# A pooling and neighbourhood-attention encoder layer on eight cores: loads of one buffer issued without order among them, and a rearranged prologue

## The chip, the cores and the metric

The kernel runs on the 8 cores of one Trainium2 chip. Each core computes one batch element, with no exchange between cores. The metric is the device time of the slowest core in microseconds; the time before is the median of 3 runs.

## The reference

One encoder layer over two inputs per core, 8192 and 2048 tokens of 1024 channels. Weights are float32 in DRAM; the kernel multiplies in bf16.

```python
xn = rmsnorm(x, norm_mix); z = xn @ w_in              # 512 p, 512 q, 512 k, 512 v, 2048 gates
g_pool, g_na = split(sigmoid(g + b_gate))
pooled = centred means (windows 2, 4, 8, 16) of p, minus p
pool_out = ((pooled @ w_pool_grp) * pool_scale) @ w_pool_proj
na_out = neighbourhood_attention(q, k, v, rpb) @ w_na_proj   # 8 heads, window 8 rows x 16 columns
x = x + (g_pool * pool_out + g_na * na_out) @ w_out
x = x + square(relu(rmsnorm(x, norm_mlp) @ w_ff1)) @ w_ff2
return rmsnorm(x, norm_final)
```

## The kernel before

**Stages.** A core's 10240 tokens are 20 stages of 512 tokens (stages 0 to 15 the long input, 16 to 19 the short one). A stage is `stage_g` (eight steps m: gate matmuls L801, tanh L806, the two projections L821, the products L825 and L829), `stage_mid` (v_part L557, w_out L874, norms, the next keys L535, p L593, q L704) and `stage_ff` (w_ff1 L937, w_ff2 L964). The attention of the next stage is laid into `stage_ff`: 16 units of head pair and query column group, each a scores matmul (L620), an exponential on ACT (L625), a product with a bias table on DVE (L629) and a values matmul (L643).

**Order of work.** There is no planner. `Prog.op` (L42) appends each instruction to the list of its engine in program order and derives semaphore waits from the keys that it reads and writes. So every engine, and every queue of DMA issues (SP, ACT, POOL), is in order. Two DMAs that write one key get a wait between them: the second is issued when the first has landed. This holds for the two halves of a gate block (`cast_block`, L272), for the two halves of column block 0 in `v_gather` (L571), and for the parts of a bias table in `tab_set` (L378).

**Weights.** All weights pass through a ring of five slots of 1 MB (`wring`), in the order of the list `order`. The first uses of a block are cast from float32 DRAM by POOL (L274); at use number `keep_at` the block is stored to `wbs` by ACT's queue (`keep_block`, L277), and later uses are loaded by SP (L433). BK, BV, BP and BQ are kept at their second use, which falls into stage 0; the blocks of w_ff at the second or third. A slot is filled again when its block has been used and stored. BPP, the pooling projection, is folded with w_pool_grp and pool_scale by `fold` (L1085) into xn2T, and stored.

**Bias tables.** `t_load` brings rpb strips into gsc (two at a time), `t_exp` exponentiates them into xr, `t_masks` makes masks (in xa), and `t_prod` (L346) multiplies: 6 products a kind. `t_kind(2)` is made in `tab[:, 1]`; kinds 0, 3 and 1 are made in `arena`; each is stored to `tabd`. `t_first` makes the half of kind 0 that the first stage needs. `tab_set` loads what the next stage needs.

**Prologue.** It loads six x tiles, norms and transposes them, makes k, v, p and q (`k_back`, `v_part`, `p_back`, `q_proj`), and then runs the first attention alone, with one unit a step, the values two steps behind, and PSUM pairs 0, 4 and 6. `t_kind(0)`, `pooling(0)`, `t_kind(3)` and `fold` are put in at steps 2, 4 to 6, 8 and 10; `t_kind(1)` follows. x tiles 6 and 7 are loaded after it, since the masks lie in xa.

The functions that the diff touches:

## Time and profile before

| | us |
|---|---|
| median of 3 runs | 4442.44 (4439.35 to 4630.74) |
| profiled execution, its own time | 4432.12 |
| its span, first to last instruction, slowest core | 4430.5 |
| spans of the 8 cores | 4394.7 to 4430.5 |
| busy: PE, DVE, ACT, POOL | 4243.8, 2046.5, 1406.4, 481.6 |

Times in rows are microseconds from the start of the span on the slowest core (core 7). PE is the matmul engine, PEld its weight load, DVE the vector engine, ACT the scalar engine, POOL GpSimd; SPq, ACTq are issues of DMAs by those engines. L801 is line 801 of the kernel before. DMA share is the mean busy share of the core's 16 DMA engines. PEclk is the granted clock of PE, 1.00 at the higher of its levels.

### The profile page before, as it was taken

What the parts mean: (1) busy time and instruction counts of PE and PEld (TensorE: products, weight loads), DVE (VectorE), ACT (ScalarE), POOL (GpSimd) and SP (SyncE); (2) the same over time, 40 slices, a digit from 0 to 9 for tenths busy, and PEclk for the clock granted to TensorE, in tenths of its full rate; (3) what the DMA queues carried; (4) which work ended last, traced back from release to release, by engine and by line L of the source; (5) the groups of instructions that cost most, each with busy time, mean ns of one, the idle gap of its engine ahead of it and who ended that gap; (6) DMA issues with size and microseconds to landing.
All of it is one profiled execution on the core that took longest, in us unless ns stands there. A gap on an engine that the chain in (4) does not pass through costs nothing.

```text
span 4430.5 us, 65741 instructions; the slowest of 8 cores (4394.7 to 4430.5 us)
## 1 busy us (share of the span) xinstructions
PE 4243.8 (96%) x23436; PEld 2067.1 (47%) x23436; DVE 2046.5 (46%) x3041; ACT 1406.4 (32%) x2153; POOL 481.6 (11%) x624
## 2 busy tenths in 40 slices
PE   4689899999999999999999999999999999999999
PEld 2334444444444444444444444444444444444544
DVE  3534435344444444444444454544555444444543
ACT  2323323233332333333333332323333232333321
POOL 1021202010101010110101010101010101010100
PEclk8789999999999999999999999999999999999999
DMA  9798887854454544454545454544545454545443
GB/s 177 192 204 179 174 185 203 226 195 172 176 185 156 196 162 174 168 196 164 188 157 194 149 200 159 191 170 176 197 169 179 176 180 177 198 162 180 165 163 123
DMA packets 201832, 790.53 MB, mean 178 GB/s; under 512 B 16360, under 2 KB 99304, under 8 KB 132520
## 3 DMA queue, kind: packets, MB, share of 16 engines
q1 hardware_dynamic: 133352, 695.98, 44.5%
q0 software_dynamic: 64128, 60.99, 10.3%
q10 hardware_dynamic: 4032, 29.36, 1.7%
q8 instruction: 193, 3.16, 0.3%
q14 instruction: 127, 1.04, 0.1%
HBM read 758.47 MB, written 88.78 MB: 191 GB/s over the span
## 4 chain that ended last, share of the span: by engine, by line
PE 89%; DMA 7%; DVE 2%; issue 1%; ACT 1%; SPq 0%; POOL 0%; DVEq 0%; ACTq 0%; POOLq 0%
PE psum L964 24%; PE psum L937 24%; PE psum L801 11%; PE psum L874 6%; PE psum L821 6%; PE psum L620 3%; PE psum L557 3%; PE psum L535 3%; PE psum L704 3%; PE psum L593 3%; PE psum L643 2%; DMA wring<-w_ff 2%; DMA vtok<-vd 1%; PE psum L493 1%; DMA gsc<-rpb 1%
## 5 line engine op out<-in xcount | busy, mean ns | idle before, releaser
L964 PE MATMUL psum<-wring,arena 128*128 128x512 bf16 x5120 | 1160.5, 380 | 12.6 <-DMA wring<-w_ff 12.6
L937 PE MATMUL psum<-xn2T,wring 128*128 128x512 bf16 x5120 | 1163.8, 381 | 4.4 <-DMA wring<-w_ff 3.4
L964 PEld LDWEIGHTS psum<-wring,arena 128*128 128x128 bf16 x5120 | 491.1, 98 | 553.1 <-issue 21.0
L937 PEld LDWEIGHTS psum<-xn2T,wring 128*128 128x128 bf16 x5120 | 492.4, 98 | 547.4 <-issue 16.8
L944 DVE TENSOR_TENSOR arena<-rl 128x512 bf16<-128x512 f32 x640 | 473.2, 741 | 578.0 <-ACT rl L942 577.1
L942 ACT ACTIVATE rl<-psum 128x512 f32<-128x512 f32 x640 | 382.3, 597 | 762.5 <-PE psum L937 603.8
L801 PE MATMUL psum<-xnT,wring 128*128 128x512 bf16 x2560 | 607.8, 380 | 0.0
L625 ACT ACTIVATE pTs<-psum 128x1024 bf16<-128x1024 f32 x320 | 327.4, 1023 | 837.1 <-PE psum L620 810.2
L969 DVE TENSOR_TENSOR xr<-psum,xr 128x512 f32<-128x512 f32 x320 | 221.3, 692 | 621.1 <-PE psum L964 613.2
L472 POOL TENSOR_SCALAR var<-ssq 128x1 f32<-128x1 f32 x240 | 66.8, 278 | 3255.2 <-ACT xs L469 3251.5
L806 ACT ACTIVATE gsc<-psum,hbT 128x512 f32<-128x512 f32 x320 | 218.9, 686 | 541.3 <-PE psum L801 504.2
L801 PEld LDWEIGHTS psum<-xnT,wring 128*128 128x128 bf16 x2560 | 250.3, 98 | 298.9 <-issue 2.8
L629 DVE TENSOR_TENSOR pTs<-pTs,tab 128x1024 bf16<-128x1024 bf16 x320 | 240.9, 753 | 212.4 <-ACT pTs L625 212.4
L825 DVE SCALAR_TENSOR_TENSOR gsc<-gsc,psum 128x512 f32<-128x512 f32 x320 | 216.6, 685 | 235.8 <-PE psum L821 123.4
L874 PE MATMUL psum<-wring,arena 128*128 128x512 bf16 x1280 | 291.7, 387 | 24.3 <-DMA wring<-w_out 11.4
L469 ACT ACTIVATE xs<-xr 128x1024 bf16<-128x1024 f32 x160 | 168.4, 1054 | 226.4 <-DVE xr L969 130.7
L874 PEld LDWEIGHTS psum<-wring,arena 128*128 128x128 bf16 x1280 | 126.0, 99 | 178.4 <-issue 37.0
L620 PE MATMUL psum<-qbd,kT 128*128 128x256 bf16 x1280 | 198.6, 279 | 9.1 <-DVE qbd L466 6.7
L643 PE MATMUL psum<-vtok,pTs 128*128 128x65 bf16 x2560 | 133.5, 196 | 58.8 <-DVE pTs L629 27.3
L475 POOL TENSOR_TENSOR rstd<-var,nhalf 128x1 f32<-128x1 f32 x240 | 183.6, 765 | 37.7 <-POOL var L472 3.4
L643 PEld LDWEIGHTS psum<-vtok,pTs 128*128 128x128 bf16 x2560 | 122.0, 99 | 139.1 <-issue 72.0
L821 PE MATMUL psum<-arena,wring 128*128 128x512 bf16 x640 | 164.2, 379 | 14.9 <-ACT gsc L806 14.9
(88 smaller groups left out, 3036.1 us busy)
## 6 DMA issues: line engine op xcount, KB each, us to landing
wring<-wbs SPq DMA_DIRECT2D x483, 1024.0 KB, 6.0
wring<-w_ff POOLq DMA_DIRECT2D x42, 1024.0 KB, 18.9
xr<-x SPq DMA_DIRECT2D x80, 512.0 KB, 9.0
y<-xr SPq DMA_DIRECT2D x80, 512.0 KB, 3.7
xa<-x SPq DMA_DIRECT2D x76, 512.0 KB, 6.8
wbs<-wring ACTq DMA_DIRECT2D x27, 1024.0 KB, 11.3
xn2T<-wbs SPq DMA_DIRECT2D x19, 1024.0 KB, 7.4
vd<-vst SPq DMA_DIRECT2D x19, 520.0 KB, 8.4
```

Of the source, the lines that this page charges most:

```text
L620: ins = e.matmul(out=pb(pair + rb, lr * 256, lr * 256 + 256), lhsT=kT[:, m, ks, cb, :], rhs=qbd[:, m, g, :, :], start=True, stop=True)
L625: P.op("act", lambda e: e.activation(out=pTs[:, pslot, :], in_=psum[:, pair * 512:pair * 512 + 1024], func=AF.Exp, scale=0.125), reads=["p ...
L629: P.op("dve", lambda e: e.tensor_tensor(out=pv_, in0=pv_, in1=tab[:, :, v0:v0 + 2, 2 * m:2 * m + 2, :].rearrange("p r v h q -> p r v (h q) ...
L643: ins = e.matmul(out=pb(bo, ocol, ocol + 65), lhsT=pTs[:, pslot, base:base + 128], rhs=vtok[:, ks, cb, h, :], start=(i == 0), stop=(i == 3))
L801: ins = e.matmul(out=pb2(b), lhsT=WG[:, k, col0:col0 + 128], rhs=xn(u0, k), start=(k == 0), stop=(k == 7))
L821: ins = e.matmul(out=pb(b2), lhsT=Wp[:, k, m * 128:(m + 1) * 128], rhs=src[:, k, :], start=(k == 0), stop=(k == 3))
L874: ins = e.matmul(out=pb(b), lhsT=mT[:, k, tl * 128:(tl + 1) * 128], rhs=W[:, k, :], start=(k == 0), stop=(k == 7))
L937: ins = e.matmul(out=pb(b), lhsT=W[:, k, c4 * 128:(c4 + 1) * 128], rhs=xn2T[:, k, :], start=(k == 0), stop=(k == 7))
L942: P.op("act", lambda e, b=b, rs_=rs_: e.activation(out=rl[:, rs_, :], in_=pb(b), func=AF.Relu), reads=["ps%d" % b], writes=["rl%d" % rs_])
L944: P.op("dve", lambda e, rs_=rs_, hc=hc: e.tensor_tensor(out=hidT[:, hc, :], in0=rl[:, rs_, :], in1=rl[:, rs_, :], op=ALU.mult), reads=["rl ...
L964: ins = e.matmul(out=pb(b), lhsT=hidT[:, kg * 8 + k, tl * 128:(tl + 1) * 128], rhs=W[:, k, :], start=(kg == 0 and k == 0), stop=(kg == 1 a ...
L969: P.op("dve", lambda e, b=b, xv=xv: e.tensor_tensor(out=xv, in0=pb(b), in1=xv, op=ALU.add), reads=["ps%d" % b, "xr%d" % tl], writes=["xr%d ...
```

## The change

Four things are changed. (1) `op` takes `joined`: such a DMA does not wait for others on its own semaphore. It is used for the later parts in `cast_block`, `v_gather` and `tab_set`. (2) BK, BV, BP and BQ are kept at their first use, in the prologue. (3) The masks move out of xa into xr and arena, kinds are all made in `tab`, kinds 1, 3 and 0 in the first `stage_g` after steps m = 0, 1 and 3, each stored by `t_keep`; since kinds 0 and 1 are then in place, stage 0 reloads no table. (4) Loads and prologue are reordered: six x tiles first, strips and small constants behind; wgn, BQ, BPP, and x tiles 6 and 7 before `k_back`; `t_exp(0)` and `(1)` after it, `t_exp(2)` and `(3)` after v; `q_proj` ahead of `t_kind(2)`; `fold` ahead of the first attention, in which only the pooling is left, one operation list entry per step from step 3.

```diff
-    def op(self, eng, fn, reads=(), writes=(), dsem=None):
+    def op(self, eng, fn, reads=(), writes=(), dsem=None, joined=False):
...
+        own = self.dsems[dsem][0] if joined else None
...
             s, v, clk = tok
+            if s is own:
+                return
...
-        for (vf, src) in block_srcs(b):
+        for i, (vf, src) in enumerate(block_srcs(b)):
             P.op("pool", lambda e, vf=vf, src=src: e.dma_start(out=vf(dst), in_=src, max_dma_last_dim=8192),
-                 writes=[wkey], dsem=wkey)
+                 writes=[wkey], dsem=wkey, joined=i > 0)
...
-    masks = xaf[:, 0:1536].bitcast(BF16).rearrange("p (k v q) -> p k v q", k=4, v=6)
+    masks = [(xr[:, 3, 384 * k:384 * k + 384].bitcast(BF16) if k < 2 else arena[:, 4608 + 768 * k:5376 + 768 * k])
+             .rearrange("p (v q) -> p v q", v=6) for k in range(4)]
+    MSK = ["mk%d" % k for k in range(4)]
...
     def t_kind(k):
+        rb = (0, 1, 1, 0)[k]
         for v in range(6):
-            t_prod(k, dst, keys, 0, 128, v)
+            t_prod(k, tab[:, rb], ["tab%d" % rb], 0, 128, v)
+
+    def t_keep(k):
+        rb = (0, 1, 1, 0)[k]
+        P.op("sp", lambda e: e.dma_start(out=tabd[k], in_=tab[:, rb].rearrange("p v h q -> p (v h q)")),
+             reads=["tab%d" % rb], writes=["tabd%d" % k], dsem="tabd%d" % k)
...
-                        reads=["tabd%d" % k], writes=[key], dsem=key)
+                        reads=["tabd%d" % k], writes=[key], dsem=key, joined=key in begun)
+                    begun.add(key)
...
-    keep_at.update({b: 1 for b in (BK, BV, BP, BQ)})
...
-                    reads=["vd%d" % blk] + (["vd0"] if blk == 0 else []), writes=["vtok%d_%d" % (ks, cb)], dsem="vt%d_%d" % (ks, cb))
+                    reads=["vd%d" % blk] + (["vd0"] if blk == 0 else []), writes=["vtok%d_%d" % (ks, cb)], dsem="vt%d_%d" % (ks, cb),
+                    joined=lo > 0)
...
-    x_load(0)
-    load(g1b[:], norm_mix.partition_broadcast(128), "g1b")
-    x_load(1)
-    x_load(2)
-    x_load(3)
+    for j in range(6):
+        x_load(j)
+        if j == 0:
+            load(g1b[:], norm_mix.partition_broadcast(128), "g1b")
+    t_load(0)
+    t_load(1)
+    load(psT[:], pool_scale, "psT")
     load(mrow[:], c_mrow, "mrow")
     load(mcol[:], c_mcol, "mcol")
-    t_load(0)
-    t_load(1)
-    x_load(4)
-    x_load(5)
+    load(bgT[:], b_gate, "bgT")
+    load(pfac[:], c_fac, "pfac")
...
     p_norm(1)
-    ws_fill(1)
     a_tr(0)
     p_norm(2)
     a_tr(1)
     p_norm(3)
-    t_first_zero()
     ws_fill(1)
-    t_exp(0)
-    t_exp(1)
-    t_load(2)
-    t_load(3)
+    P.op("pool", lambda e: e.dma_start(out=wgn, in_=w_grp.rearrange("g c d -> c g d"), max_dma_last_dim=8192), writes=WGN, dsem="wgn")
+    ws_fill(2)
+    for j in (6, 7):
+        a_load(j)
...
         p_norm(5)
-        t_exp(2)
-        t_exp(3)
         a_tr(4)
         a_tr(5)
+        t_first_zero()
         t_masks()
     k_back([0, 1], rest)
-    P.op("pool", lambda e: e.dma_start(out=wgn, in_=w_grp.rearrange("g c d -> c g d"), max_dma_last_dim=8192), writes=WGN, dsem="wgn")
+    t_exp(0)
+    t_exp(1)
+    t_load(2)
+    t_load(3)
...
-    load(psT[:], pool_scale, "psT")
-    load(bgT[:], b_gate, "bgT")
-    load(pfac[:], c_fac, "pfac")
+    t_exp(2)
+    t_exp(3)
...
     t_first()
+    q_proj(0)
     t_kind(2)
-    q_proj(0)
+    t_keep(2)
...
+    fold()
     reserved.update((2, 3))
     P.fence("act", ["xp4", "xp5"])
     plan = att_plan(0, 1, 2, [0, 4, 6])
-    plan[2].append(lambda: t_kind(0))
-    plan[4].append(lambda: pool_fin.extend(pooling(0)))
-    plan[6].append(lambda: [f_() for f_ in pool_fin])
-    plan[8].append(lambda: t_kind(3))
-    plan[10].append(fold)
+    for i, f_ in enumerate(sum(pooling(0), [])):
+        plan[i + 3].append(f_)
...
-    t_kind(1)
+    tab_now.update({(0, 0): 0, (0, 1): 0, (1, 0): 1, (1, 1): 1})
+    g_hooks[0] = [lambda: t_kind(1), lambda: t_keep(1)]
+    g_hooks[1] = [lambda: t_kind(3), lambda: t_keep(3)]
     g_hooks[2] = [lambda: keep_block(xn2f, BPP, "xn2T")]
+    g_hooks[3] = [lambda: t_kind(0), lambda: t_keep(0)]
     load(g2b[:], norm_mlp.partition_broadcast(128), "g2b")
     load(nfb[:], norm_final.partition_broadcast(128), "nfb")
-    for j in (6, 7):
-        a_load(j)
```

## Rows read from the trace of the kernel before

**Rows 1.** The page, busy tenths in 40 slices of the span (DMA: mean share)

```profile
PE   4689899999999999999999999999999999999999
...
DMA  9798887854454544454545454544545454545443
```

**Rows 2.** Timeline of PE, first gate matmuls of stages; start us, us, form

```profile
164.77 3.62 PE L801 MATMUL psum<-xnT,wring 128*128 128x512 bf16 x8
...
415.34 1.89 PE L801 MATMUL psum<-xnT,wring 128*128 128x512 bf16 x8
...
649.85 1.89 PE L801 MATMUL psum<-xnT,wring 128*128 128x512 bf16 x8
...
1080.46 1.89 PE L801 MATMUL psum<-xnT,wring 128*128 128x512 bf16 x8
...
1290.11 1.89 PE L801 MATMUL psum<-xnT,wring 128*128 128x512 bf16 x8
...
3388.90 1.89 PE L801 MATMUL psum<-xnT,wring 128*128 128x512 bf16 x8
...
3608.77 1.89 PE L801 MATMUL psum<-xnT,wring 128*128 128x512 bf16 x8
```

**Rows 3.** Stretches: length, busy PE PEld DVE ACT POOL, PEclk, DMA share, GB/s

```profile
120.00:150.00 30.00, 11.91 (x88) 7.14 (x88) 20.51 (x39) 8.24 (x10) 0.86 (x1) 0.53 0.33 115
300.00:390.00 90.00, 88.69 (x526) 44.09 (x524) 43.23 (x68) 29.50 (x43) 13.47 (x14) 1.00 1.08 156
480.00:640.00 160.00, 140.62 (x793) 68.89 (x792) 63.47 (x92) 44.98 (x67) 25.54 (x24) 0.93 1.00 186
```

**Rows 4.** Timeline of PE, its waits; in brackets idle before and its releaser

```profile
109.59 0.60 PE L643 MATMUL psum<-vtok,pTs 128*128 128x65 bf16 x8 [14.03 <-DVE pTs L629]
...
236.51 3.57 PE L874 MATMUL psum<-wring,arena 128*128 128x512 bf16 x8 [5.06 <-DMA wring<-w_out]
...
293.03 0.60 PE L643 MATMUL psum<-vtok,pTs 128*128 128x65 bf16 x8 [3.94 <-DMA vtok<-vd]
...
519.23 0.60 PE L643 MATMUL psum<-vtok,pTs 128*128 128x65 bf16 x8 [12.22 <-DMA vtok<-vd]
...
633.93 3.57 PE L964 MATMUL psum<-wring,arena 128*128 128x512 bf16 x8 [7.17 <-DMA wring<-w_ff]
...
3443.27 3.57 PE L874 MATMUL psum<-wring,arena 128*128 128x512 bf16 x8 [5.53 <-DMA wring<-wbs]
```

**Rows 5.** Timeline of DVE in the first attention, same columns

```profile
81.90 10.92 DVE L348 TENSOR_TENSOR tab<-xr,xa 64x1024 bf16<-64x1024 bf16 x14
...
108.15 0.17 DVE L1083 TENSOR_SCALAR hbT<-bgT 128x16 f32<-128x16 f32 x1 [12.78 <-DMA bgT<-b_gate]
...
112.87 4.67 DVE L348 TENSOR_TENSOR arena<-xr,xa 128x1024 bf16<-128x1024 bf16 x6
...
143.28 1.45 DVE L1095 TENSOR_SCALAR rl<-psum,psT 128x128 bf16<-128x128 bf16 x4
...
150.18 0.69 DVE L466 CAST xn2T<-psum 128x512 bf16<-128x512 f32 x1 [0.78 <-ACT xn2T L464]
```

**Rows 6.** Timelines of POOL and of ACT, same columns

```profile
29.97 0.96 POOL L274 DMA_DIRECT2D wring<-w_in  x1 [10.95 <-issue]
...
200.82 1.06 ACT L469 ACTIVATE xs<-xa 128x1024 bf16<-128x1024 f32 x1 [9.06 <-DMA xa<-x]
```

**Rows 7.** DMA queues from 165 to 620: packets, MB, share of 16 engines

```profile
q0 software_dynamic: 39013, 39.35, 63.7%
q1 hardware_dynamic: 8013, 32.23, 22.5%
```

**Rows 8.** Chain that ended last, in order of time: start us, us, what

```profile
282.21 10.68 DMA vtok<-vd
...
504.05 14.94 DMA vtok<-vd
```

**Rows 9.** Timeline of SP's queue: start us, us from first issue to last

```profile
3417.50 15.38 SPq L401 DMA_DIRECT2D tab<-tabd  x5
```

More of the change, by code:

```diff
@@ L312, in build_nc @@
     VST = ["vst%d" % c for c in range(6)]
-    xaf = xa[:].rearrange("p a b -> p (a b)")
-    masks = xaf[:, 0:1536].bitcast(BF16).rearrange("p (k v q) -> p k v q", k=4, v=6)
-    XA = ["xa0", "xa1"]
+    masks = [(xr[:, 3, 384 * k:384 * k + 384].bitcast(BF16) if k < 2 else arena[:, 4608 + 768 * k:5376 + 768 * k])
+             .rearrange("p (v q) -> p v q", v=6) for k in range(4)]
+    MSK = ["mk%d" % k for k in range(4)]
     expb = xr[:].rearrange("p a b -> p (a b)")[:, 0:3072].bitcast(BF16).rearrange("p (h q) -> p h q", h=24)
@@ L334, in t_masks @@
                 P.op("dve", lambda e, k=k, v0=v0, v1=v1, ty=ty: e.tensor_tensor(
-                    out=masks[:, k, v0:v1, :].rearrange("p v (r q) -> p v r q", q=16),
+                    out=masks[k][:, v0:v1, :].rearrange("p v (r q) -> p v r q", q=16),
                     in0=mrow[:, k, ty, :].unsqueeze(1).unsqueeze(3).broadcast_to([128, v1 - v0, 8, 16]),
                     in1=mcol[:, v0:v1, :].unsqueeze(2).broadcast_to([128, v1 - v0, 8, 16]), op=ALU.mult),
-                    reads=["mrow", "mcol"], writes=XA)
+                    reads=["mrow", "mcol"], writes=[MSK[k]])
     def ex_view(o, rb):
@@ L349, in t_prod @@
             out=dst[lo:lo + n, v], in0=ex_view(VAR_OFF[v], rb)[lo:lo + n],
-            in1=masks[lo:lo + n, k, v, :].unsqueeze(1).broadcast_to([n, 8, 128]), op=ALU.mult),
-            reads=EXPB + XR4 + XA, writes=keys)
+            in1=masks[k][lo:lo + n, v, :].unsqueeze(1).broadcast_to([n, 8, 128]), op=ALU.mult),
+            reads=EXPB + XR4 + [MSK[k], "hid12", "hid13", "hid14"], writes=keys)
     def t_kind(k):
-        if k == 2:
-            dst, keys = tab[:, 1], ["tab1"]
-        else:
-            dst = arena[:, 0:6144].rearrange("p (v h q) -> p v h q", v=6, h=8)
-            keys = HID
-        for v in range(6):
-            t_prod(k, dst, keys, 0, 128, v)
-        P.op("sp", lambda e: e.dma_start(out=tabd[k], in_=dst.rearrange("p v h q -> p (v h q)")),
-             reads=keys, writes=["tabd%d" % k], dsem="tabd%d" % k)
+        rb = (0, 1, 1, 0)[k]
+        for v in range(6):
+            t_prod(k, tab[:, rb], ["tab%d" % rb], 0, 128, v)
[3 more added lines that the diff above has]
+             reads=["tab%d" % rb], writes=["tabd%d" % k], dsem="tabd%d" % k)
     def t_first_zero():
@@ L374, in t_first @@
             t_prod(0, tab[:, 0], ["tab0"], 96, 32, v)
-    tab_now = {(0, 0): None, (0, 1): 0, (1, 0): 2, (1, 1): 2}
+    tab_now = {}
     def tab_set(first, last):
@@ L391, in tab_set @@
             todo += [(rb,) + p_ for p_ in parts]
+        begun = set()
         for zero in (True, False):
@@ L739, in pooling, with sum2, double @@
         eng = "dve" if s == 0 else "pool"
-        P.op(eng, lambda e: e.tensor_tensor(out=sm, in0=p(1, 4, -8, 526), in1=p(1, 4, -7, 526), op=ALU.add),
-             reads=win, writes=GSC)
-        for i, d in enumerate((2, 4, 8)):
-            n = (524, 520, 512)[i]
-            P.op(eng, lambda e, i=i, d=d, n=n: e.tensor_tensor(out=sm[:, i:3, 0:n], in0=sm[:, i:3, 0:n],
-                                                                in1=sm[:, i:3, d:d + n], op=ALU.add),
+        def sum2():
+            P.op(eng, lambda e: e.tensor_tensor(out=sm, in0=p(1, 4, -8, 526), in1=p(1, 4, -7, 526), op=ALU.add),
+                 reads=win, writes=GSC)
+        def double(i):
+            d, n = (2, 4, 8)[i], (524, 520, 512)[i]
+            P.op(eng, lambda e: e.tensor_tensor(out=sm[:, i:3, 0:n], in0=sm[:, i:3, 0:n],
+                                                in1=sm[:, i:3, d:d + n], op=ALU.add),
                  reads=GSC, writes=GSC)
+        sums = [sum2] + [lambda i=i: double(i) for i in range(3)]
         def fin0():
@@ L763, in fin @@
                 op0=ALU.mult, op1=ALU.add), reads=win + GSC, writes=["pooledT"])
-        return [fin0] + [lambda g=g: fin(g) for g in range(1, 4)]
+        return sums, [fin0] + [lambda g=g: fin(g) for g in range(1, 4)]
     def x_res(s):
@@ L909, in stage_mid @@
             q_proj(s + 1)
-            pool_fin[:] = pooling(s + 1)
+            sums, pool_fin[:] = pooling(s + 1)
+            for f_ in sums:
+                f_()
     def stage_ff(s):
@@ L1010, in build_nc @@
     ws_fill(2)
-    P.op("dve", lambda e: e.memset(nhalf[:], -0.5), writes=["nhalf"])
-    x_load(0)
-    load(g1b[:], norm_mix.partition_broadcast(128), "g1b")
-    x_load(1)
-    x_load(2)
-    x_load(3)
+    for j in range(6):
[5 more added lines that the diff above has]
+    load(psT[:], pool_scale, "psT")
     load(mrow[:], c_mrow, "mrow")
     load(mcol[:], c_mcol, "mcol")
-    t_load(0)
-    t_load(1)
-    x_load(4)
-    x_load(5)
+    load(bgT[:], b_gate, "bgT")
+    load(pfac[:], c_fac, "pfac")
     P.op("dve", lambda e: e.memset(xnT[:, :, 0:256], 0.0), writes=["xnT0"])
```

## The prediction

> **What bounds the kernel now.** I read the 40 slices first [rows 1]. PE is at 9 tenths from the sixth slice on; the first five (some 550 us) hold 4, 6, 8, 9, 8. The DMA line stands at 7 to 9 through the first eight and then falls to 4 and 5. So two regimes: a start in which the DMA engines are full, and a steady part bound by PE. Next the first gate matmul of each stage, from the timeline of PE [rows 2]. Between 1080.46 and 1290.11 a stage takes 209.7 us; that is PE's own length, and what a stage takes beyond it is what could be gained. The prologue ends at 164.8. Stage 0 takes 415.3 - 164.8 = 250.5 (40.8 beyond), stage 1 649.8 - 415.3 = 234.5 (24.8 beyond), stage 15 219.9 (10.2); the next is of the same pattern (8.0). These two are the ones that reload bias tables in parts. Third, the stretches [rows 3]: at 120 to 150 PE is busy 11.9 of 30 us at half clock (0.53) while DMA is at 0.33, DVE is busiest (20.5); at 300 to 390 and 480 to 640 DMA is at 1.08 and 1.00, no room. Last the waits of PE in the timeline [rows 4] and DVE's own line through the first attention [rows 5].
>
> **Prologue and first attention.** Before, the first values matmul waits 14.03 us for DVE and starts at 109.59 [rows 4], because DVE sat 12.78 us on b_gate, whose load was queued behind the gathers, until 108.15 [rows 5]. After, b_gate is loaded at the head, so that wait is gone, but other things stand there. In DVE's new order are: the eight products of t_first and six of t_kind(2) (10.92 us for the 14, [rows 5]), with q's four copies (2.5 us) between; fold's four scalings (1.45) and its eight copies of xn2T, a chain that alternates ACT and DVE and takes 0.73 us a link and 5.9 in all, the last at 150.18; then scores, exp and product, some 3 us. Sum 23.8 us, with hbT 24. It starts when p's copies are done, 81.9 before. That now waits for t_exp(2) and t_exp(3), which stand ahead of them on ACT and whose bias strips can only be loaded once t_exp(0) and (1) have freed gsc, after k_back; DVE then also has t_first_zero (4.6) and t_masks (6.2) between the two K blocks, so k's last copy goes from 61 to about 64, t_exp(0) ends at 65.5, two loads of 0.75 MB take 10 to 14 us there, and p's copies end at 87. 87 + 24 = 111 for the first values matmul, 1.5 us later than before. So the b_gate wait is not gained; it is refilled.
>
> The gain is in the attention. It took 164.8 - 109.6 = 55.2 us. Two t_kinds of 4.67 us and fold (143.28 to 150.87 with PE's part and the stall behind it, 10 us) stood in DVE's line [rows 5]; with lag 2 and three PSUM pairs little of that is hidden. 55.2 - 9.3 - 10 = 36. The pooling, spread over eight units where it came in two lumps, hides some 3 us more: 33. Prologue end 111 + 33 = 144, **-21 us**. Bounds: if the strips land early and DVE's other work hides, 133 (-32); if they land as t_load did in a full queue, and POOL holds the norms of tiles 4 and 5 behind BPP, 158 (-7). That POOL can be held is in the row at 29.97: the fourth cast of a block waited 10.95 us with nothing before it but queue space [rows 6]; now wgn, BQ and BPP all stand before those two norms. I take 2 us for it, within the 87.
> K, V, P, Q are stored to wbs already here: four stores of 1 MB, 3.3 us of all DMA engines each (below). They delay slots 0 to 3, but the casts of BG0 to BG2 are due only at 144, and DMA was idle for two thirds of 120 to 150 [rows 3]; hidden by that.
>
> **Stage 0.** Price of DMA work from 165 to 620 [rows 7]: the software queue (casts) 39.35 MB in 63.7% of 455 us, 7.4 us per MB, 7.7 per block of 1.05 MB; the hardware queue 32.23 MB in 22.5%, 3.2 per MB, 3.3 per block. BV, BK, BP, BQ become plain loads: 4 x 4.4 = 18 us less, their stores are past: 13 less; no table reload (2.36 MB): 7.5 less; tiles 6 and 7 loaded in the prologue: 3 less; tables 1, 3 and 0 are written here, where only 1 was: 2 x 1.57 MB, 10 more. Net 31 us of DMA work less, in a stage where the share was full to 390. Now place by place, against 40.8 us excess. (a) Gates: 214.7 - 164.8 = 49.9 for 41.4 of work; 6 us were the waits for tiles 6 and 7, the table product and slow clock. After, three t_kinds of 4.67 us stand in DVE's line after m = 0, 1 and 3, and the third writes the buffer that t_keep(3) is still reading (7 to 13 us for 1.5 MB), so DVE waits some 4 us, with the products of m = 4 and the evacuations behind it. PE runs two m ahead through 8 banks; I leave 5 us of stall, gain 1 to 2. (b) v_part and w_out: PE waited 2.4 us, then 5.06 at 236.51 and 6.36 at the one like it before, and ran eight matmuls twice in 3.57 us where 1.73 is full speed, 17.5 in all [rows 4]. BWO0 was late because its slot waited for the store of BG1, whose issue sat on ACT behind the norm of a late tile; that one goes. BWO1 stays: ACT still waits for tile 8 (9.06 us before [rows 6], loaded behind t_keep(3) on SP now), so the store of BG2 lands at +42 and the cast 16 to 20 us later, against a need at +50. I leave 10 us, gain 7.5. (c) The gather: PE waited 3.4 + 3.9 us around 280 to 293 for the second half of a pair that was issued when the first had landed (10.7 us later [rows 8]); joined, both land together. With the clock (6.35 and 6.15 us for 16 matmuls, 3.45 at speed) 13 us, of which 12 go. **-21 us** (a + b + c, 20.5 to 21.5). Is DMA ready? Before, BWO's release at 250 to the last ff cast at 392 was 142 us, with 11 us to spare at the end; PE now needs 13 less, DMA has 5 to 6 less there. It just fits, and from here the bound is close. Bounds -8 to -34.
>
> **Stage 1.** The same gather costs 12.22 us at 519.23, the longest wait [rows 4], the second half landing 14.94 us after the first [rows 8]. But 480 to 640 is full of DMA: 16 casts x 7.7 = 123, six stores and some loads of 3.3, together about 155 of 160 us, and PE waits again at 633.93, 7.17 us, for the last ff blocks. Taking 12 us out moves that wait up, it does not remove it: what is gained is the DMA idle time that PE's stall made (520 to 530), **-4 us**, bounds 0 and -16.
>
> Here the Trainium skill speaks otherwise. The last rows have a gather half of 65 KB landing 10.7 us after issue in a full queue [rows 8]. "DMA: Bandwidth & Descriptors" (Anatomy of one DMA) fits a DMA with 2.0 us plus bytes over 436 GB/s. An estimate by that page is 2.2 us for the half, so joining would give 2 us a stage, and a block of 1 MB would take 4.4, so that 16 would fit well under PE. By it stage 0's gather would give 2 us instead of 12, and the sum be 10 less there and up to 8 more in stage 1. The rows decide; the rest stands on them.
>
> **Stages 15 and 16, and all others.** At 3417.5 SP needs 15.38 us to issue five table loads [rows 9], each waiting for the one before; the wring load behind them makes PE wait 5.53 us at 3443.27 with 3.57 for eight matmuls [rows 4] (the same at 3663). Joined, five issues take 3 us, so the load goes 12 us earlier: 7.5 each, **-15 us** (bounds -10, -17). In the other stages SP is freed for 4.5 us each, and nothing waits there: 0.
> Sum -21 -21 -4 -15 = -61: 4432.1 - 61 = 4371 of this execution, whose span is 4430.5. The median of the runs shown is 10.3 us higher; the prediction is for that: 4442.4 - 61, 4381.
>
> **Rivals.** (1) DMA takes it back. Work moved forward meets casts that can't come sooner: stage 0's last blocks are late by what the front gained. For it: DMA 1.08 to 390 [rows 3]. Against: 31 us less work, and idle time at 120 to 150 that can be used. The prologue's 21 stays half, stage 0 gives 5: -10 -5 -0 -15 = -30, 4412. (2) All of it comes through: prologue -32, stage 0 -34, stage 1 -14 (casts not the bound), tables -17: -97, 4345. The fit of the Trainium skill above would have it so for the casts. For it: the waits that go are there in full, 14.03, 3.94 and 12.22 us [rows 4]. Against: the wait for w_ff at 633.93. (3) The joined loads do not help, since the second half lands when it did anyhow, in a queue that is served in turn: -61 + 12 + 4 + 5 = -40, 4402. (4) Slower. One mechanism: a slot can be refilled only after its block was stored, the stores are issued by ACT, and ACT sits on strips loaded late; then BG1 to BG3 are late in the gates, and every later block in a ring without slack. A hold of ACT for one late tile was 9.06 us [rows 6]; nine such landing on PE (four slots in the gates, five while the ring catches up in stages 0 and 1) are 81.5. It decides from the seventh on, 61 us: -61 + 81 = +20, 4462. DMA's idle 120 to 150 speaks against it.
>
> **Chances.** Forecast 0.60, (1) 0.16, (2) 0.14, (3) 0.07, (4) 0.03. The range is 4345 to 4422: it takes in (1), (2) and (3). A measurement here tells 2% (89 us) from no change: faster by that is under 4353.6, most of (2) and a little of the forecast, 0.13; slower 0.02; within 0.85.
>
> **What would show it.** First values matmul at 111 with no 12.78 us wait for b_gate; gates from 144; attention 33 us; b_gate, fold and two t_kinds outside it. PE's wait for w_out once, near 10 us. In stage 0 no wait for vtok over 3 us; in stage 1 vtok gone and the w_ff wait near 634 grown to 15 or more after the shift. SP's five table loads in 3 us and no wait at stages 15 and 16. It is wrong if gates start after 155, if stage 1 takes under 222 us (then casts did not bind), or if stage 0 stays over 240.

## The result, and the profile after

The changed kernel takes 0.989 of the time before (95% interval 0.986 to 0.993): 48 us less of 4442, between 33 and 63. The prediction was 61 us less. The medians of all runs are 4396.34 and 4536.59 us; executions in which the cores of a die ran at a lower clock pull the second one up, and the ratio leaves them out. The profiled execution took 4394.56 us (before 4432.12), its span is 4392.7 us, on core 1.

The page after, the same lines as [rows 1]:

```profile
PE   5689989899999999999999999999999999999999
...
DMA  9898988845454545454545454545455554545443
```

The first slices are fuller (5, 6, 8, 9, 9 against 4, 6, 8, 9, 8), and the DMA line of the first eight is as full as it was. The steady part is the same. The first gate matmuls of the stages, as in [rows 2] (L808 is L801 before):

```profile
149.88 3.62 PE L808 MATMUL psum<-xnT,wring 128*128 128x512 bf16 x8
...
395.07 1.89 PE L808 MATMUL psum<-xnT,wring 128*128 128x512 bf16 x8
...
626.79 1.89 PE L808 MATMUL psum<-xnT,wring 128*128 128x512 bf16 x8
...
851.15 1.89 PE L808 MATMUL psum<-xnT,wring 128*128 128x512 bf16 x8
...
1060.94 1.89 PE L808 MATMUL psum<-xnT,wring 128*128 128x512 bf16 x8
...
3369.09 1.89 PE L808 MATMUL psum<-xnT,wring 128*128 128x512 bf16 x8
...
3580.46 1.89 PE L808 MATMUL psum<-xnT,wring 128*128 128x512 bf16 x8
```

Prologue 149.9 (164.8 before), stage 0 245.2 (250.5), stage 1 231.7 (234.5), stage 2 224.4 (220.9), a steady stage 209.8 still, stage 15 211.4 (219.9).

The slowest core is not the same one in every trace, and stages 0 to 2 differ from core to core by up to 20 us (stage 1 before: 214.7 to 234.5), so the experiments are read by the median over the eight cores, taken from the same first gate matmuls in each core's trace:

| medians over 8 cores, us | prologue | stage 0 | 1 | 2 | 15 | 16 | slowest span |
|---|---|---|---|---|---|---|---|
| before | 161.9 | 253.7 | 221.7 | 220.8 | 218.2 | 217.7 | 4430.5 |
| changed | 149.9 | 243.2 | 227.0 | 221.4 | 211.4 | 210.0 | 4392.7 |
| e1_before_joined | 159.0 | 256.3 | 223.8 | 221.6 | 211.4 | 209.9 | 4415.2 |
| e2_after_unjoined | 149.1 | 248.3 | 226.6 | 221.9 | 216.4 | 217.4 | 4423.0 |
| e3_early_stores | 149.8 | 239.2 | 229.9 | 218.8 | 211.4 | 209.9 | 4387.9 |
| e4_no_table_stores | 151.0 | 231.4 | 229.5 | 222.3 | 211.4 | 209.9 | 4384.8 |
| e6_late_keep | 148.5 | 259.3 | 223.4 | 221.3 | 211.4 | 210.0 | 4401.2 |
| e7a_after_ff_plain | 148.4 | 244.1 | 209.7 | 209.7 | 211.4 | 209.9 | 4358.5 |
| e7b_before_ff_plain | 163.2 | 255.5 | 209.7 | 209.7 | 217.8 | 217.4 | 4405.5 |
| e8_early_strips | 143.6 | 245.7 | 229.9 | 219.7 | 211.4 | 210.0 | 4386.9 |
| e9_keep_split | 149.5 | 255.1 | 214.9 | 211.9 | 211.4 | 209.9 | 4381.3 |
| e10_three | 144.5 | 247.5 | 211.8 | 211.8 | 211.4 | 209.9 | 4369.9 |
| e11_three_half | 145.6 | 262.0 | 209.7 | 209.7 | 211.4 | 209.9 | 4376.0 |
| e12_four | 145.3 | 232.4 | 214.4 | 211.8 | 211.4 | 209.9 | 4368.0 |

By it the change gave 12 us in the prologue and 10.5 in stage 0, lost 5.3 in stage 1 and 0.6 in stage 2, and gave 14.5 in stages 15 and 16. The rest is mostly the slowest core: before, the latest of the eight was 11.6 us behind the median core (4430.5 against 4418.9), after, 6.7. A median hides where the cores fall into two groups; where they do (e9, e10, e12), the text says so.

**The prologue.** Timeline of DVE after, where [rows 5] was:

```profile
86.63 0.42 DVE L469 CAST pTb<-psum 128x256 bf16<-128x256 f32 x1 [13.82 <-ACT pTb L467]
...
90.29 6.22 DVE L351 TENSOR_TENSOR tab<-xr 64x1024 bf16<-64x1024 bf16 x8
...
99.09 4.67 DVE L351 TENSOR_TENSOR tab<-xr,arena 128x1024 bf16<-128x1024 bf16 x6
...
103.88 1.46 DVE L1104 TENSOR_SCALAR rl<-psum,psT 128x128 bf16<-128x128 bf16 x4
...
111.35 0.69 DVE L469 CAST xn2T<-psum 128x512 bf16<-128x512 f32 x1 [0.78 <-ACT xn2T L467]
```

The 12.78 us wait for b_gate is gone, and what has taken its place is the 13.82 us wait for p's copies on ACT. Then follow t_first (6.22), q's copies, t_kind(2) (4.67), fold's scalings, and the copies of xn2T, the last at 111.35. ACT waited itself, for the strips (timeline of ACT):

```profile
80.07 1.49 ACT L330 ACTIVATE xr<-gsc 128x1536 bf16<-128x1536 f32 x1 [9.11 <-DMA gsc<-rpb]
84.78 1.48 ACT L330 ACTIVATE xr<-gsc 128x1536 bf16<-128x1536 f32 x1 [3.23 <-DMA gsc<-rpb]
```

and POOL was held at the issue of a cast, as in the row at 29.97 of [rows 6], here twice: 10.25 us before 30.48, and then (timeline of POOL):

```profile
45.80 0.75 POOL L277 DMA_DIRECT2D wring<-w_pool_proj  x1 [14.43 <-issue]
```

The cast of BPP waited 14.43 us with two norms behind it. The profile names no releaser, but by the trace's landings both casts went out 0.3 us after an earlier one had landed (30.14 and 45.49), which is what a wait for queue space looks like. The first of the two norms reached DVE at 47.73, where tile 4's stood at 43.70 before.

**PE's waits** after, for [rows 4] (timeline of PE, in brackets the idle time before and its releaser):

```profile
115.79 0.60 PE L647 MATMUL psum<-vtok,pTs 128*128 128x65 bf16 x8 [1.63 <-DVE pTs L633]
...
209.17 3.03 PE L560 MATMUL psum<-wring,xnT 128*128 128x512 bf16 x8 [3.68 <-DVE gsc L832]
...
230.22 3.57 PE L881 MATMUL psum<-wring,arena 128*128 128x512 bf16 x8 [15.34 <-DMA wring<-w_out]
...
276.31 0.40 PE L647 MATMUL psum<-vtok,pTs 128*128 128x65 bf16 x8 [1.42 <-DMA vtok<-vd]
...
523.06 3.57 PE L973 MATMUL psum<-wring,arena 128*128 128x512 bf16 x8 [5.29 <-DMA wring<-w_ff]
...
611.75 3.57 PE L973 MATMUL psum<-wring,arena 128*128 128x512 bf16 x8 [10.22 <-DMA wring<-w_ff]
```

The first values matmul is at 115.79, 6.2 us later than before. The second w_out block makes PE wait 15.34 us. The gathers cost 1.42 us in stage 0 and nothing in stage 1, where the w_ff blocks cost 5.29 and 10.22. That is not the slowest core alone: in stage 1 before, all eight cores waited for vtok, 3.2 to 12.2 us, and three of them for w_ff (7.2, 7.1 and 0.8 us); after, one waits for vtok (1.6 us at most), and all of them for w_ff, 8.1 to 10.9 us at the last blocks. In stage 0 the waits for w_out come to as much as before: 15.5 us before in the median over the cores, in two waits, and 15.3 after, on most cores in one. The slowest core of the kernel before had the smallest sum of the eight, 11.4 us. Where the 15.34 us come from, in the chain that ended last:

```profile
171.91 16.33 DMA xa<-x
...
188.71 15.53 DMA wbs<-wring
...
204.98 25.10 DMA wring<-w_out
```

Tile 8 loads for 16.3 us, the store of BG2 that ACT issues after it takes 15.5, the cast into the slot 25.1. ACT's wait for the tile (timeline of ACT):

```profile
188.61 1.06 ACT L472 ACTIVATE xs<-xa 128x1024 bf16<-128x1024 f32 x1 [13.69 <-DMA xa<-x]
```

And the stretches (columns as in [rows 3]):

```profile
150.00:165.00 15.00, 15.00 (x59) 6.27 (x58) 7.48 (x12) 4.82 (x9) 0.72 (x2) 0.83 0.25 99
165.00:180.00 15.00, 15.00 (x82) 7.26 (x81) 11.27 (x16) 3.71 (x6) 2.19 (x4) 1.00 1.02 299
180.00:195.00 15.00, 9.42 (x33) 3.52 (x32) 8.49 (x12) 5.18 (x9) 0.79 (x2) 0.81 1.04 279
195.00:210.00 15.00, 11.32 (x50) 4.91 (x49) 4.16 (x7) 2.65 (x4) 1.75 (x3) 0.96 1.02 266
210.00:225.00 15.00, 4.22 (x14) 1.19 (x12) 3.69 (x6) 0.00 (x0) 0.00 (x0) 0.73 1.02 290
```

DMA stands at 0.25 in the first 15 us of the gates and then at 1.02 to 1.04 for 60 us. SP's queue at stage 15, for [rows 9]:

```profile
3397.68 3.09 SPq L404 DMA_DIRECT2D tab<-tabd  x5
3401.60 11.55 SPq L436 DMA_DIRECT2D wring<-wbs  x3
```

Five table loads in 3.09 us instead of 15.38, and no wait of PE behind them.

### The profile page after: what moved, and what is told of

The parts are those of the page before. It is cut to its first block, busy times and chain, and to the rows that moved or that the text cites. A ratio compares the mean times of both kernels' runs of the same rounds, so it can differ in the third digit from the quotient of the medians.

```text
span 4392.7 us, 65696 instructions; the slowest of 8 cores (4370.4 to 4392.7 us)
## 1 busy us (share of the span) xinstructions
PE 4227.1 (96%) x23436; PEld 2061.6 (47%) x23436; DVE 2048.1 (47%) x3040; ACT 1406.2 (32%) x2153; POOL 479.4 (11%) x620
## 3 DMA queue, kind: packets, MB, share of 16 engines
q14 instruction: 127, 1.04, 0.1%
## 4 chain that ended last, share of the span: by engine, by line
PE 91%; DMA 5%; issue 2%; DVE 2%; ACT 1%; POOL 0%; ACTq 0%; SPq 0%; DVEq 0%; POOLq 0%
PE psum L973 25%; PE psum L946 23%; PE psum L808 12%; PE psum L881 6%; PE psum L828 6%; PE psum L538 3%; PE psum L624 3%; PE psum L708 3%; PE psum L560 3%; PE psum L597 3%; DMA wring<-w_ff 2%; PE psum L647 2%; PE psum L496 2%; DMA wbs<-wring 1%; DMA wring<-w_out 1%
## 5 line engine op out<-in xcount | busy, mean ns | idle before, releaser
L808 PE MATMUL psum<-xnT,wring 128*128 128x512 bf16 x2560 | 608.5, 381 | 2.3 <-ACT gsc L813 2.3
L808 PEld LDWEIGHTS psum<-xnT,wring 128*128 128x128 bf16 x2560 | 250.5, 98 | 302.6 <-issue 7.4
L881 PE MATMUL psum<-wring,arena 128*128 128x512 bf16 x1280 | 284.4, 381 | 17.9 <-DMA wring<-w_out 15.3
L828 PE MATMUL psum<-arena,wring 128*128 128x512 bf16 x640 | 164.2, 379 | 18.2 <-ACT gsc L813 14.9
L485 DVE SCALAR_TENSOR_TENSOR xs<-xr,rstd,g2b 128x1024 bf16<-128x1024 f32 x80 | 102.7, 1284 | 143.6 <-POOL rstd L478 140.1
## 6 DMA issues: line engine op xcount, KB each, us to landing
wbs<-wring ACTq DMA_DIRECT2D x27, 1024.0 KB, 11.6
```

The lines of the kernel that those rows point to most:

```text
L808: ins = e.matmul(out=pb2(b), lhsT=WG[:, k, col0:col0 + 128], rhs=xn(u0, k), start=(k == 0), stop=(k == 7))
L828: ins = e.matmul(out=pb(b2), lhsT=Wp[:, k, m * 128:(m + 1) * 128], rhs=src[:, k, :], start=(k == 0), stop=(k == 3))
L881: ins = e.matmul(out=pb(b), lhsT=mT[:, k, tl * 128:(tl + 1) * 128], rhs=W[:, k, :], start=(k == 0), stop=(k == 7))
```

## The experiments

The question after the trace: stage 0 gave 5 to 10 us where 21 were forecast, and stage 1 got longer in the median. Is the second w_out block late because its slot is held (theory D, the way the prediction had worked it out), or because the queues are full (E)? And do the casts of w_ff take back what comes before them (A)?

**e1_before_joined, e2_after_unjoined: the joined loads alone, and all the rest alone.** The edit of e1 is the hunks of the change that have `joined` in them. e2:

```diff
-            if s is own:
-                return
```

> The kernel before with the joined loads alone (gate block halves, gathers, table parts), nothing moved. Theory A (my forecast's steps): the gather wait of stage 0 goes, stage 0 is 10 to 13 us shorter; stage 1 only 0 to 5 shorter, its 12 us wait for vtok comes back as waits for w_ff; stages 15 and 16 are 8 us shorter each; in all -26 to -34 us. Rival B (casts don't bind in the ff phase): stage 1 is 12 to 15 us shorter as well, in all -40 or more. Rival C (joining gives nothing, the second half lands when it did): stages 0, 15 and 16 as before, in all 0 to -5.

> The changed kernel with every joined load waiting for the one before again. Theory A: the prologue is hardly later (first gate matmul within 4 us of 149.9), stage 0 is 8 to 12 us longer, stage 1 within 4 us, stages 15 and 16 8 us longer each, in all +22 to +32 us against the changed kernel, which leaves it 10 to 20 us faster than before. Rival C: within 5 us of the changed kernel.

e1 takes 0.994 of the time before (0.992 to 0.996), 27 us less; e2 0.996 (0.994 to 0.998), 18 us less. Together 45 of the 48: within the intervals the two halves add up. Stages 15 and 16 are as expected, 14.6 us in the medians, and in e2 both rows are back (SP's queue, then PE, at stage 15):

```profile
3410.82 17.03 SPq L402 DMA_DIRECT2D tab<-tabd  x5
```

```profile
3437.76 3.57 PE L879 MATMUL psum<-wring,arena 128*128 128x512 bf16 x8 [6.70 <-DMA wring<-wbs]
```

But stage 0 of e1 missed: 256.3, no shorter than before. Its gather wait is gone, and another has grown (timeline of PE in stage 0 of e1):

```profile
229.87 3.57 PE L880 MATMUL psum<-wring,arena 128*128 128x512 bf16 x8 [17.33 <-DMA wring<-w_out]
...
293.94 0.40 PE L649 MATMUL psum<-vtok,pTs 128*128 128x65 bf16 x8 [0.57 <-DMA vtok<-vd]
```

PE waits 17.33 us for the first w_out block. Over the eight cores this wait is 12.5 to 17.3 us, where it was 6.4 to 9.7 before. In e1's trace SP issues its five table loads at 189.73 within 3.88 us, and the cast of that block goes out behind them at 194.31. That the loads then stand in the queues ahead of it, and that the two edits are better together because the changed kernel has no such loads in stage 0, is argued from these two times and from the medians over the cores (the cast goes out 34.3 us after the start of the gates, 33.7 before, and lands at 68.2, where it was 62.3); it was not tried alone. e2's stage 0 is 5.1 us longer than the changed kernel's, not 8 to 12.

**e3_early_stores, e4_no_table_stores: slot held, or queues full.** The edit of e3:

```diff
+    def keep_ahead(b):
+        kept.add(b)
+        slot = ws["slot_of"][order.index(b)]
+        keep_block(wring[:, slot, :], b, "wr%d" % slot)
...
-        if b != BPP and uses[b] - 1 == keep_at[b]:
+        if b != BPP and uses[b] - 1 == keep_at[b] and b not in kept:
...
+        if s == 0:
+            keep_ahead(BG[1])
+            keep_ahead(BG[2])
```

e4 drops the three `t_keep` calls from the hooks and puts them into stage 6; what is stored for kind 3 is then kind 0, so the tables of the last stages of each input are wrong.

> The changed kernel with the stores of gate blocks BG1 and BG2 issued by ACT at the start of the first gates instead of when each block is taken up. Theory D (w_out is late because its slot waits for a store that ACT issues only after it has sat on the late tile 8): the cast of the second w_out block is issued about 183 to 186 instead of 205, PE's 15.3 us wait for it falls to 0 to 3, stage 0 is 12 to 16 us shorter unless the casts of w_ff then bind; total -8 to -16. Rival E (DMA throughput: table stores and tiles fill the queues): the cast is issued earlier but lands late, the wait falls by less than 6 us, total 0 to -5.

> The changed kernel with the three table stores taken out of the first gates and put into stage 6, where the buffers hold other kinds: what is stored there is wrong, and the tables of the last stages with it. All products stay. Theory D: tile 8 is loaded as early as the gathers of DVE let it, ACT's 13.7 us on it falls to about 9, DVE's 4.5 us wait for the store of kind 3 goes, PE's wait for w_out falls by some 5 us, stage 0 is 6 to 10 us shorter. Rival E: 13.5 us of DMA work less ahead of the w_out casts takes the whole 15 us wait and more away, stage 0 is 14 us shorter or more.

e3 takes 0.989 of the time before (0.987 to 0.991), the same as the changed kernel; e4 0.988 (0.985 to 0.991), which can't be told from it. In e3 the cast was issued 15.7 us earlier (POOL), 3 to 6 us later than D had it, since the norm of tile 8 stands ahead of it on POOL. But PE waits as long (PE):

```profile
189.32 0.96 POOL L277 DMA_DIRECT2D wring<-w_out  x1
```

```profile
206.71 1.89 PE L893 MATMUL psum<-wring,arena 128*128 128x512 bf16 x8 [2.68 <-DMA wring<-w_out]
224.62 3.57 PE L893 MATMUL psum<-wring,arena 128*128 128x512 bf16 x8 [16.02 <-DMA wring<-w_out]
```

189.32 to 224.62 is 35 us in the queue, where it was 25.1. The cast was issued 15.7 us earlier and the block landed 5.6 us earlier; stage 0 is 4.0 us shorter in the median, stage 1 2.9 longer and stage 2 2.6 shorter. D, as it was worked out (wait near zero), falls. In e4 the cast was issued earlier too, 13.1 us (191.87), and here the block landed 13.7 us earlier, 216.47 for 230.22:

```profile
216.47 3.20 PE L881 MATMUL psum<-wring,arena 128*128 128x512 bf16 x8 [14.84 <-DMA wring<-w_out]
```

```profile
210.00:225.00 15.00, 8.53 (x46) 4.13 (x47) 2.77 (x4) 2.06 (x3) 0.79 (x2) 0.69 0.45 118
```

At 210 to 225 the share is down to 0.45. The slowest core is another one in each run, so here are the same two times as medians over the eight cores, with two later runs:

| second w_out block of stage 0, us after the first gate matmul | cast issued | landed |
|---|---|---|
| before | 46.9 | 72.0 |
| changed | 52.3 | 77.6 |
| e3_early_stores | 39.6 | 73.7 |
| e4_no_table_stores | 39.7 | 66.0 |
| e10_three | 46.7 | 70.7 |
| e12_four | 36.4 | 66.9 |

So the same advance of the cast, 12.7 and 12.6 us, passes by a third where the other DMA work stays (e3, 3.9 us), and nearly in full where three table stores are gone (e4, 11.6 us). Three stores of 1.57 MB are some 15 us of DMA work by [rows 7]; the expectation had 13.5. e4 alone would not tell the theories apart, since its cast was early as well; the pair does. E expected e4's wait to go, and it did not: 14.84 us. PE had got there some 13 us earlier itself (201.6 for 214.9), since ACT's wait for tile 8 and DVE's for the store were shorter too. Stage 0 is 11.8 us shorter, somewhat less than the work, and stages 1 and 2 were 3.4 us longer together, so of 12 us 8 were left.

**e7a_after_ff_plain, e7b_before_ff_plain: do the casts bind stages 1 and 2.** The edit, in both kernels:

```diff
-            if order[:i].count(b) <= keep_at[b] and b != BPP or b == BPP:
+            if b >= 12 and order[:i].count(b):
+                P.op("sp", lambda e, slot=slot: e.dma_start(out=wring[:, slot, :], in_=wbs[BG[0]]),
+                     reads=["wbs%d" % BG[0]], writes=["wr%d" % slot], dsem="wl%d" % slot)
+            elif order[:i].count(b) <= keep_at[b] and b != BPP or b == BPP:
...
-        if b != BPP and uses[b] - 1 == keep_at[b]:
+        if b < 12 and b != BPP and uses[b] - 1 == keep_at[b]:
```

> The changed kernel in which every use of a w_ff block after the first is a plain load of another block already stored, and no w_ff block is stored: what the MLP of stages 1 to 19 computes is wrong, the amount of bf16 loaded is that of the steady stages. Theory A (the casts of w_ff bind stages 1 and 2, and take there what the front gained): stages 1 and 2 fall from 227 and 221 us (medians over the cores) to 210 to 213. Stage 0 keeps its 16 casts and stays at 240 to 245. Rival F (stage 1 and 2 are long for another reason, the norms, the attention or the clock): they stay over 218.

> The kernel before with the same w_ff loads (same part wrong). Theory A: stage 1 holds its gather wait here (nothing gives it back), so it stays 6 to 15 us over 209.7; stage 2 falls to 210 to 213; against the changed kernel with the same loads the difference is larger than the 48 us of the two kernels as they are: -50 to -60 us. Rival F: the same 40 to 50 us.

First gate matmuls of stages 1, 2 and 3 in e7a, then of 1 and 2 in e7b (timelines of PE):

```profile
396.08 1.89 PE L811 MATMUL psum<-xnT,wring 128*128 128x512 bf16 x8
...
605.83 1.89 PE L811 MATMUL psum<-xnT,wring 128*128 128x512 bf16 x8
...
815.48 1.89 PE L811 MATMUL psum<-xnT,wring 128*128 128x512 bf16 x8
```

```profile
429.68 1.89 PE L804 MATMUL psum<-xnT,wring 128*128 128x512 bf16 x8
...
639.39 1.89 PE L804 MATMUL psum<-xnT,wring 128*128 128x512 bf16 x8
```

Both stages take 209.7 us in the median over the cores, in both kernels. So all of the 17 and 12 us that they are over the steady length in the changed kernel is the casts and stores of w_ff. The edit takes away their DMA work and POOL's issuing of them at once, so that it is the work, and not the way of issue, is argued: from the DMA share of 1.00 with the casts [rows 3] and from e9 below. The expectation for e7b missed in one thing, and it is the most telling: its gathers still wait for each other, and yet stage 1 has no gather wait.

```profile
480.00:640.00 160.00, 160.00 (x929) 79.50 (x927) 70.12 (x111) 51.93 (x78) 15.19 (x18) 1.00 0.43 155
```

PE is busy 160.00 of 160 us, with DMA at 0.43. The 12.22 us of [rows 4] were a small load behind casts, not the price of a load that waits for another. Changed against before with these loads: 0.983 and 0.994, 10 thousandths or 46 us, no more than between the two kernels as they are; 50 to 60 was expected. The expectations for the stages of e7a held (stage 0 is 244.1).

**e8_early_strips: does a shorter prologue come through.**

```diff
     p_norm(3)
+    t_exp(0)
+    t_exp(1)
+    t_load(2)
+    t_load(3)
     ws_fill(1)
...
     k_back([0, 1], rest)
-    t_exp(0)
-    t_exp(1)
-    t_load(2)
-    t_load(3)
+    t_exp(2)
+    t_exp(3)
...
-    t_exp(2)
-    t_exp(3)
     slot, wkey = ws_acquire(BP)
```

> The changed kernel with t_exp(0), t_exp(1), t_load(2), t_load(3) ahead of the K blocks, and t_exp(2), t_exp(3) right behind them. If the strips' late loads cost the prologue what the profile shows (ACT 9.1 + 3.2 us for rpb, PE 4.3 us for p's copies), the first gate matmul comes 5 to 9 us earlier, 141 to 145 in the median; the total falls by less than that, 0 to 5, if the casts of stages 0 to 2 bind, and by all of it if they don't.

ACT exponentiates the strips at 24 to 30, while it has nothing else, and after the K blocks without a wait (ACT); the gates begin earlier (PE):

```profile
24.35 1.48 ACT L330 ACTIVATE xr<-gsc 128x1536 bf16<-128x1536 f32 x1 [6.42 <-DMA gsc<-rpb]
...
66.10 2.86 ACT L330 ACTIVATE xr<-gsc 128x1536 bf16<-128x1536 f32 x2
```

```profile
144.91 3.62 PE L808 MATMUL psum<-xnT,wring 128*128 128x512 bf16 x8
```

The prologue is 6.3 us shorter in the median. Stages 0 to 2 together are 3.7 us longer, so by the sum of the medians 2.6 came through by the start of stage 3, as A has it (3.8 by the median of the eight start times themselves). There is no ratio for this run, and a gain of that size would not show in one.

**e6_late_keep: the four stores in the prologue.** The edit puts `keep_at.update({b: 1 for b in (BK, BV, BP, BQ)})` back.

> The changed kernel with BK, BV, BP and BQ stored at their second use again (as before the change). Theory A: the prologue is 0 to 3 us shorter (no stores in a full queue, no slot waits for them), and stage 0 6 to 12 us longer, since four casts and four stores return to it: total +3 to +9. Rival: early keeping is worth nothing or costs, total 0 to -5.

0.992 (0.989 to 0.995), some 12 us slower than the changed kernel by the ratios, though their intervals overlap; the median core is 8.5 us later (4394.5 against 4386.0). The prologue is 1.4 us shorter and stage 0 16.1 longer, more than the 6 to 12 expected: four casts for four loads and four stores, some 30 us of work put where no room is. Of all parts undone this one costs stage 0 most: without it the stage would be longer than before the change (259.3 for 253.7).

**e9_keep_split, e10_three, e11_three_half: less DMA work.** If the start of stage 3 is set by DMA work, the way to gain is to take work away. A block of w_ff stored at its first use costs one store in stage 0 and saves one or two casts after it. e9:

```diff
-        keep_at[12 + n_] = 1 if n_ % 3 == 0 else 2
+        keep_at[12 + n_] = (0, 1, 2, 1, 2, 1, 2, 0)[n_ % 8]
```

e10 is that with the edit of e8 and with `t_keep(1)` and `t_keep(0)` moved from stage 0's hooks to stage 6, where their buffers still hold these kinds. e11 is e10 with `n_ % 2`.

> The changed kernel with the stores of the 16 w_ff blocks split over three stages: 4 at the first use, 6 at the second, 6 at the third (before: 6 at the second, 10 at the third). Theory A (total DMA work up to the start of stage 3 sets when stage 3 starts): 4 more stores in stage 0 (4 x 2.7 us), in stage 1 four casts with or without store and in stage 2 eight casts less. Stage 1 falls from 227 to 211 to 217 us, stage 2 from 221 to 210 to 214, stage 0 rises by 3 to 11; total -10 to -20 against the changed kernel. Rival (only the burst in each ff phase counts, stores in stage 0 cost more than they return): total -5 to +5.

> The same split, with the strips loaded and exponentiated early, and with the stores of bias table kinds 1 and 0 put off to stage 6 (their buffers hold them until stage 14, so nothing is left out). Theory A: prologue 143 to 145 us, two table stores of three out of stage 0 (8 of the 12 us that taking out three gave), stages 1 and 2 as in the split alone: total -22 to -32 against the changed kernel, near 4365. Rival: as the split alone, -10 to -20, since the front's gains are taken back again.

> As the last, but 8 blocks stored at the first use and 8 at the second. Theory A: stage 2 is 209.7 us, stage 1 210 to 212, stage 0 6 to 11 us longer than with four stores: total within 6 us of the last, to either side.

e9: 0.986 (0.983 to 0.988), 16 us less than the changed kernel by the ratios, whose intervals overlap; the times themselves, taken on two chips, do not (4373.21 to 4383.53 against 4386.15 to 4398.11). Stage 1 is 214.9, stage 2 211.9, as expected, and stage 0 is 11.9 us longer in the median, a little over the 3 to 11 expected. But the median stands for no core: on two of the eight stage 0 is 241.8 and 242.5, no longer than in the changed kernel, and on six it is 253.1 to 258.5. The six wait 6 to 9 us for one of the last w_ff blocks of the stage, the two don't. e10: 0.984 (0.981 to 0.986), 25 us less than the changed kernel, in the range expected, and again 0.984 (e10b_three, the same kernel). There too stage 0 has two short cores (234.7 and 237.1) and six long ones (242.9 to 251.6). e11: 0.985 (0.983 to 0.987): stages 1 and 2 are at 209.7, and stage 0 is 14.5 us longer than e10's, where 6 to 11 were expected; all eight cores are long (260.0 to 265.9) and wait 20 to 22 us for w_ff blocks. In e10 PE waits in stage 0 for w_out and at the end of w_ff:

```profile
216.21 3.57 PE L881 MATMUL psum<-wring,arena 128*128 128x512 bf16 x8 [13.84 <-DMA wring<-w_out]
...
380.88 3.57 PE L973 MATMUL psum<-wring,arena 128*128 128x512 bf16 x8 [7.71 <-DMA wring<-w_ff]
```

**e12_four, e10b_three: the question of e3 again, with room in the queues.** e10 and the edit of e3.

> The run with three changes (e10) and the early stores of BG1 and BG2 (e3) on top. Theory E (DMA work ahead of the second w_out block sets when it lands; early stores only use the idle DMA of the first gates, 0.34 share at 150 to 165): PE's wait for w_out stays 9 to 15 us, the landing comes 3 to 7 us earlier, stage 0 is 3 to 6 us shorter of which the ff casts take back some; total -2 to -5 against e10. Theory D (the held-up store): with two table stores gone the queues have room at 210 to 225 (0.45), so the wait falls by 8 us or more, total -8.

> The same kernel as e10, for a comparison on the same chip as e12: 0.98 to 0.986 of the kernel before.

```profile
180.91 0.96 POOL L277 DMA_DIRECT2D wring<-w_out  x1
```

```profile
212.44 3.57 PE L893 MATMUL psum<-wring,arena 128*128 128x512 bf16 x8 [14.55 <-DMA wring<-w_out]
```

The cast was issued 10.5 us earlier than in e10, the block landed 3.8 us earlier, and PE's wait is 14.55 us. E again: a third of the advance passed. Stage 0 is 15 us shorter in the median over the cores (232.4), which neither theory expected. It is the two groups again: five cores are short now (230.3 to 233.0, no wait for a w_ff block), where e10 had two, and three are long (245.2 to 248.1, with 8.0 to 8.3 us of such a wait near the end of the stage). So the earlier block may have taken three more cores past that wait, with which a core's stage is some 14 us longer in all; whether it is the cause is open, since one profiled execution can't show that it would be so again. The slowest span, 4368.0, is a long core's and 1.9 us from e10's. e12 takes 0.982 (0.978 to 0.986), e10b on the same chip 0.984 (0.981 to 0.986): they can't be told apart. Both beat the kernel before; their intervals end where the changed kernel's begins, at 0.986.

## Why the prediction was right or wrong

The sum was -61 and -48 was measured. The mechanisms of the prologue and of the table loads were right; one step of stage 0 was not.

**Prologue, -21 forecast, -14.9 on the slowest core (-12.0 in the median).** The mechanism was right and the attention itself too: 149.9 - 115.8 = 34.1 us for a forecast of 33, with two t_kinds and fold taken out of it. The first values matmul was due at 111 and came at 115.8. Two terms were too small: p's copies were done at 90.3, not 87, since the strips were waited for until 84.78 and POOL held the norms 4 us instead of 2; and the chain behind them took 25.5 us, not 24. That b_gate's wait would be refilled rather than gained was right.

**Stage 0, -21 forecast, -5.3 on the slowest core (-10.5 in the median).** By a sign that the prediction named itself (wrong if stage 0 stays over 240) it was wrong here: 245.2. The step that failed is (b), v_part and w_out, a gain of 7.5 us. I had read the lateness of the second w_out block as a chain of issue times (late tile, store, cast) and left 10 us of 17.5. In that chain the store of BG2 was to land 42 us after the start of the gates, the cast 16 to 20 us behind it, and PE to be there at 50. Measured, the store landed at 54.4 (issued at 38.8, in the queue for 15.5), the cast was 25.1 us in the queue and landed at 80.2, and PE was there at 65.0. From the first v_part matmul to the end of that block's first eight matmuls it is 30.2 us, where it was 25.4 (medians over the cores 28.5 and 26.9). So 2 to 5 us were lost where 7.5 were to be gained.

What the chain had too short is the time that a transfer stays in full queues. The issue time counts, but only by a third (e3, e12: medians of 12.7 and 10.3 us of advance gave 3.9 and 3.8); with the table stores gone nearly the whole advance came through (e4). So the landing is set mostly by the other DMA work then in the queues, and there the change puts two more table stores. The 31 us of DMA work that I had counted as gone did go, and the count was right: the share over stage 0 is 1.00 of 250.6 us before and 0.89 of 245.2 us after, 32 us less. But much of it went at times when DMA was then idle (0.25 at 150 to 165) because the five slots were full (POOL's next cast, at 173.06, waited for PE's gates to free one), and up to the start of stage 3 nothing went: 0.88 of 870.7 us before, 0.90 of 851.1 us after, some 766 us of work each time. The change moved DMA work ahead; e9 takes some away (0.86 of 839.1 us, some 720).

(a) failed too, 53.7 us for the gates instead of 48 to 49: DVE waited 4.54 us for the store of kind 3 as forecast, but ACT 13.69 us for tile 8. (c) has the right size, 1.42 us of wait are left, but one of its rows was misread: of the 3.4 + 3.9 us put down to the gather, the first is a wait for a w_ff block.

```profile
282.74 6.35 PE L937 MATMUL psum<-xn2T,wring 128*128 128x512 bf16 x16 [3.43 <-DMA wring<-w_ff]
```

It went too, and joining the gather in the kernel before (e1) did not shorten the stage; so the 14 us by which the stage is shorter from the w_out block on (161.3 for 175.2) are not the gather's alone. A store was priced by the wrong queue, too: ACT's stores are a hardware queue of their own, 16.43 MB in 9.5% of the 455 us of [rows 7], 2.8 us for a block and not 3.3.

**Stage 1, -4 forecast.** On the slowest cores it is -2.8; in the median over the cores +5.3. The reason given held: the wait for vtok went from 12.22 us to none, and the waits for w_ff grew from 7.17 to 15.5 ("15 or more"). e7a shows that the casts and stores of w_ff are all of it. But the prediction let stage 0 pass its gain on. Rival (1), that DMA takes back what the front gains, is in part what happened: 12 + 10.5 us gained ahead of stage 1, 5.9 taken back in stages 1 and 2, and of e8's 6.3 us 2.6 came through. The weight of 0.60 against 0.16 was too one-sided; the measured -48 lies between the -61 of the one and the -30 of the other.

**The weighing of the Trainium skill.** By an estimate from the fit in "DMA: Bandwidth & Descriptors" (Anatomy of one DMA) of the Trainium skill, 16 casts fit well under PE. No run agrees: with casts stages 1 and 2 are 12 to 17 us over, without them 209.7. The Trainium skill gives that fit for DMAs issued by GpSimd; the gather is issued by SP, so the fit was not made for it, and the 2.2 us estimated for a half were 10.68 and 14.94 us in the full queues [rows 8]. That joining is worth little in stage 1 came true all the same, for another reason: e7b shows that the unjoined pair costs PE nothing once the casts are gone.

**Stages 15 and 16, -15 forecast, -16.3 on the slowest core, -14.5 in the median.** Right in size and place: SP's 15.38 us are 3.09, and the clock's part with them. Rival (3) is out by the same rows. Rival (4) has no row: the stores ahead of the casts of the gate blocks did hold POOL (17.6 us once), and PE did not wait for one gate block.

**All other stages, 0 forecast:** 209.8 and 209.7.

## What to carry to other kernels

Where DMA engines are full over several stages, a wait in the trace names the transfer that happened to be needed, not its cause: taking an order or a late issue away moves the wait to the next transfer. Count the DMA work between two points instead, and the room that idle slots leave; edits that remove work (a block stored once instead of cast three times, a table store put off to a quiet stage) gave in these full stages what edits of order did not: e9 is 16 us under the changed kernel, e3 none, and e1's stages 0 to 2 are no shorter than before. Look at every core as well: where a wait is just missed or just met, the cores fall into two groups, and a median jumps from one to the other. And where the steady part is at its bound, look for the few stages that differ from it: two table reloads were a third of the gain for one flag.
